# Shorter mean sums, split last tiles, reordered first products and identity products in the norms of an f32 kernel

## The reference, cut to what matters

```python
def rms_norm(x, g):
    x32 = x.astype(jnp.float32)
    y = x32 * lax.rsqrt(jnp.mean(x32 * x32, axis=-1, keepdims=True) + EPS)
    return (y * g.astype(jnp.float32)).astype(x.dtype)
...
        x = x + mixed @ w_out[l]
        x = x + peer_ffn(rms_norm(x, norm2_g[l]), w_peer_q[l], peer_keys1[l], peer_keys2[l],
                         peer_u[l], peer_v[l])
```

## Time and profile before

| what | value |
|---|---|
| median of 3 runs | 2213.49 us (2211.61 to 2214.72) |
| the profiled execution's own time | 2211.12 us |
| its span, first to last instruction | 2209.3 us |
| mean granted PE clock | 0.977 of full speed |
| PE busy | 2133.0 us, 97% of the span |
| DVE, ACT busy | 1543.1 us, 1127.5 us |
| PE on the chain that ended last | 85% |

### The profile page before, as it was taken

The page is one execution under the profiler, slowest core; times in us unless marked ns, Lnnn a source line. Parts: engine busy times, 40 slices in busy tenths (PEclk is TensorE's granted clock), DMA queues, the critical chain, the costliest instruction groups (busy, mean ns, idle before and its releaser), DMA issues.

```text
span 2209.3 us, 40301 instructions
## 1 busy us (share of the span) xinstructions
PE 2133.0 (97%) x16826; PEld 2059.7 (93%) x16826; DVE 1543.1 (70%) x2684; ACT 1127.5 (51%) x1745; POOL 274.4 (12%) x256
## 2 busy tenths in 40 slices
PE   8999999999999999999999999999999999989998
PEld 7888899999998999999999999999879999989998
DVE  6777588764996777877777576573457886676664
ACT  5556578544444666554444454562245543435553
POOL 0000000001889445410000000000000000000000
PEclk9999999999999999999999999999899999999999
DMA  5433433566554444446777676322015767544563
GB/s 194 160 130 108 137 124 109 188 219 229 182 182 163 146 143 142 138 162 241 246 236 265 219 243 236 114 95 87 25 39 189 245 234 252 198 146 153 182 180 116
DMA packets 104005, 375.43 MB, mean 170 GB/s; under 512 B 11536, under 2 KB 12176, under 8 KB 103184
## 3 DMA queue, kind: packets, MB, share of 16 engines
q1 hardware_dynamic: 103824, 372.86, 50.2%
HBM read 370.71 MB, written 2.10 MB: 169 GB/s over the span
## 4 chain that ended last, share of the span: by engine, by line
PE 85%; DVE 7%; ACT 3%; POOL 2%; DMA 1%; issue 1%; SPq 0%; DVEq 0%; ACTq 0%
PE ps L365 24%; PE ps L366 23%; PE ps L367 23%; PE ps L696 3%; DVE wl L1428 2%; POOL wl L2117 2%; PE ps L449 1%; PE ps L495 1%; DMA raw<-in_ada 1%; PE ps L433 1%; PE ps L434 1%; PE ps L435 1%; PE ps L790 1%; PE ps L809 1%; ACT wh L997 1%
## 5 line engine op out<-in xcount | busy, mean ns | idle before, releaser
L365 PE MATMUL ps<-xah,wh 128*128 128x256 f32 x2944 | 850.9, 289 | 15.6 <-DVE xal L1453 5.2
L366 PE MATMUL ps<-xal,wh 128*128 128x256 f32 x2944 | 838.7, 285 | 0.0
L367 PE MATMUL ps<-xah,wl 128*128 128x256 f32 x2944 | 838.4, 285 | 0.0
L1428 DVE TENSOR_TENSOR wl<-raw,wh 128x1024 fp32r<-128x1024 f32 (+2 forms) x548 | 644.6, 1197 | 216.2 <-ACT wh L997 215.0
L997 ACT ACTIVATE wh<-raw 128x1024 fp32r<-128x1024 f32 (+1 forms) x608 | 620.1, 1036 | 300.2 <-PE ps L367 179.5
L365 PEld LDWEIGHTS ps<-xah,wh 128*128 128x128 f32 x2944 | 570.9, 194 | 27.7 <-issue 18.3
L366 PEld LDWEIGHTS ps<-xal,wh 128*128 128x128 f32 x2944 | 570.9, 194 | 0.5 <-issue 0.2
L367 PEld LDWEIGHTS ps<-xah,wl 128*128 128x128 f32 x2944 | 570.2, 194 | 0.0
L365 PE MATMUL ps<-hh,wh 128*128 128x256 f32 x1024 | 291.7, 285 | 9.5 <-DVE wl L1428 7.8
L366 PE MATMUL ps<-arenar,wh 128*128 128x256 f32 x1024 | 289.7, 283 | 0.0
L367 PE MATMUL ps<-hh,wl 128*128 128x256 f32 x1024 | 289.7, 283 | 0.0
(11 more groups left out here) (332 smaller groups left out, 2942.3 us busy)
## 6 DMA issues: line engine op xcount, KB each, us to landing
raw<-in_pu SPq DMA_DIRECT2D x128, 512.0 KB, 3.3
raw<-in_pv SPq DMA_DIRECT2D x128, 512.0 KB, 3.6
raw<-in_ada SPq DMA_DIRECT2D x96, 512.0 KB, 4.2
raw<-in_ff_up SPq DMA_DIRECT2D x88, 512.0 KB, 3.6
raw<-in_w_xbc SPq DMA_DIRECT2D x32, 512.0 KB, 3.3
raw<-in_ff_down SPq DMA_DIRECT2D x32, 512.0 KB, 3.7
raw<-in_w_z SPq DMA_DIRECT2D x16, 512.0 KB, 3.3
raw<-in_w_so SPq DMA_DIRECT2D x16, 512.0 KB, 4.1
```

Of the source, the lines that this page charges most:

```text
L365: mm(o, w0, x0, start=start, stop=False, skip_group_check=skip)
L366: mm(o, w0, x1, start=False, stop=False, skip_group_check=skip)
L367: return mm(o, w1, x0, start=False, stop=stop, skip_group_check=skip)
L1428: tt_(W.lo(i), W.raw(i), W.hi(i).bitcast(f32), ALU.subtract).then_inc(S["lowV"], 1)
```

## The change

In each norm:

- `sums` (new, DVE): slices 0 to 5 of the squares are added into slice 0 by three additions (512, 512 and 256 columns). The first is put ahead of the residual additions of tile 2, the other two ahead of those of tile 3. `mean` then multiplies only slices 0, 6 and 7: 6 matmuls, 12 records.
- `last_two` (new, PE): for `out`, `down` and `oo` the last tile's halves go to two banks, each with a signal of its own. DVE adds and ACT squares slice 6 when half 0 is full, slice 7 when half 1 is. The calls of `lows` and `halves` that belong to a bank are now made once for each half.
- `first_tiles` and `l0` issue the six products that need only the high half of a slice first, behind a wait for ACT, then the three with the low half, behind the wait for DVE.
- `keep` (new, PE): products of the identity with itself, written to a part of a bank that is not read: 2 behind slice 0 of the mean (not in nc), 3 ahead of the wait for the reciprocal and 7 ahead of the first tiles (not in nc, l0; in fin only the 2 and the 3).

```diff
+            def last_two(key, w, c, nk, x, need, between=iter(())):
+                for half in range(2):
+                    P = take((key, half))
...
+                    last.then_inc(B.full((key, half), len(W.units)), 1)
...
+            def keep(P, n, start=True):
+                for _ in range(n):
+                    mm(P[:, 256:384], ident, ident, start=start, stop=True, skip_group_check=True)
...
-                for k in range(8):
-                    t.wait_ge(*step_of(name, "sq", k))
+                for k in (0, 6, 7):
+                    t.wait_ge(*(step_of(name, "sq", k) if k else summed(name)))
...
+                    if k == 0:
+                        keep(P, idle, False)
...
             def stat(name, J, sq, ids=range(8)):
-                mean(name, J, sq, ids)
-                row(name, ids)
+                mean(name, J, sq, ids, 2)
+                row(name, ids, 3)
...
+                keep(P, 7)
                 for k in range(8):
-                    need(k)
+                    need_h, need_x = need
+                    need_h(k)
                     for n, (o, i, hi, lo) in enumerate(u):
-                        last = product(o, hi[:, k, :], lo[:, k, :], x[0][:, k, :], x[1][:, k, :], k == 0 and n != 1, k == 7, skip=True)
+                        mm(o, hi[:, k, :], x[0][:, k, :], start=k == 0 and n != 1, stop=False, skip_group_check=True)
+                        mm(o, lo[:, k, :], x[0][:, k, :], start=False, stop=False, skip_group_check=True)
+                    need_x(k)
+                    for n, (o, i, hi, lo) in enumerate(u):
+                        last = mm(o, hi[:, k, :], x[1][:, k, :], start=False, stop=k == 7, skip_group_check=True)
...
+            mean("l0", K1024, sqx, HIGH, 2)
...
+                if i == 3 and (key, 0) in B.units:
+                    for half in range(2):
+                        halves(B.units[key, half] + AHEAD)
+                        a.wait_ge(*B.is_empty((key, half)))
+                        square(name, 6 + half, x, sq)
...
+            def sums(name, sq, i):
+                if i == 2:
+                    v.wait_ge(*step_of(name, "sq", 3))
+                    tt_(sq[:, 0:2], sq[:, 0:2], sq[:, 2:4], ALU.add).then_inc(own.up(), 1)
+                if i == 3:
+                    v.wait_ge(*step_of(name, "sq", 5))
+                    v.wait_ge(own.sem, own.n)
+                    tt_(sq[:, 0:2], sq[:, 0:2], sq[:, 4:6], ALU.add).then_inc(own.up(), 1)
+                    v.wait_ge(own.sem, own.n)
+                    tt_(sq[:, 0], sq[:, 0], sq[:, 1], ALU.add).then_inc(S["norm_sum"], 1)
...
             for j in range(4):
                 P = B[("y", j)]
                 v.wait_ge(*B.is_full(("y", j)))
+                sums("l0", sqx, j)
```

More of the change, by code:

```diff
@@ L394, in tile @@
                 W.done[i] = B.is_full(key)
+            def last_two(key, w, c, nk, x, need, between=iter(())):
+                for half in range(2):
+                    P = take((key, half))
+                    for k in range(0, nk, 8):
+                        n = min(8, nk - k)
+                        i, hi, lo = unit((key, half, k), w, c + half, k * 128, n * 128, 128)
+                        for q in range(n):
+                            need(k + q)
+                            last = product(P[:, 0:256], hi[:, q, :], lo[:, q, :], x[0][:, k + q, :], x[1][:, k + q, :],
+                                           k + q == 0, k + q == nk - 1)
+                        if k + n < nk:
+                            last.then_inc(W.used(i), 1)
+                        if half == 0:
+                            next(between, None)
+                    last.then_inc(B.full((key, half), len(W.units)), 1)
+                    W.done[i] = B.is_full((key, half))
             def quarters(key, w, c, xs=None):
@@ L450, in mean, with row @@
                                   stop=k == 7, skip_group_check=True)
+                    if k == 0:
+                        keep(P, idle, False)
                 last.then_inc(B.full((name, "stat"), len(W.units)), 1)
-            def row(name, ids=range(8)):
+            def row(name, ids=range(8), idle=0):
                 P = take((name, "row"), ids)
+                keep(P, idle)
                 t.wait_ge(S["rstd"], NORMS.index(name) + 1)
@@ L497, in modulation, with slices @@
                     yield
+            def slices(name):
+                return tuple((lambda k, what=what: t.wait_ge(*step_of(name, what, k))) for what in ("h", "x"))
             def n1(k):
@@ L515, in pe @@
                 if i == 0:
-                    first_tiles((("qk", 0), "w_q", 0), (("qk", 1), "w_q", 2), XA, n1, range(6))
+                    first_tiles((("qk", 0), "w_q", 0), (("qk", 1), "w_q", 2), XA, slices("n1"), range(6))
                 elif i > 1:
@@ L645, in pe @@
             for i in range(4):
-                tile(("out", i), "w_out", 2 * i, 8, XA, mixed, between=mo)
+                (tile if i < 3 else last_two)(("out", i), "w_out", 2 * i, 8, XA, mixed, between=mo)
             W.mark("spill")
@@ L763, in pe @@
             for k in range(8):
+                t.wait_ge(*step_of("l0", "h", k))
+                for n, (o, i, hi, lo) in enumerate(u):
+                    mm(o, hi[:, k, :], XA[0][:, k, :], start=k == 0 and n < 2, stop=False, skip_group_check=True)
+                    mm(o, lo[:, k, :], XA[0][:, k, :], start=False, stop=False, skip_group_check=True)
                 l0(k)
                 for n, (o, i, hi, lo) in enumerate(u):
-                    last = product(o, hi[:, k, :], lo[:, k, :], XA[0][:, k, :], XA[1][:, k, :], k == 0 and n < 2, k == 7, skip=True)
+                    last = mm(o, hi[:, k, :], XA[1][:, k, :], start=False, stop=k == 7, skip_group_check=True)
                     if k == 7:
@@ L962, in ffn @@
                 for i in range(4):
-                    tile(("down", l, i), "ff_down", 8 * l + 2 * i, 22, XF, gated, between=late)
+                    (tile if i < 3 else last_two)(("down", l, i), "ff_down", 8 * l + 2 * i, 22, XF, gated, between=late)
             ffn(0)
@@ L1522, in dve @@
             v.wait_ge(S["ld_cst"], 16)
+            for i in (2, 3):
+                sums("n1", sq1, i)
             norm("n1", xT, lambda k: pc("norm1", k), hbuf, XA)
@@ L2069, in ffn @@
                 gated(21)
-                residual([("down", l, i) for i in range(4)], l, 40, range(0, 22, 8))
+                residual(after, [("down", l, i) for i in range(4)], l, 40, range(0, 22, 8))
             ffn(0, "od")
@@ L2100, in dve @@
             v.wait_ge(own.sem, own.n)
-            residual([("oo", i) for i in range(4)], 1, 16)
+            residual("f1", [("oo", i) for i in range(4)], 1, 16)
             ffn(1, "fin")
```

61 lines of the change are left out of this document (36 added, 25 removed).

## The result

| | before | changed |
|---|---|---|
| median of the runs | 2212.21 us (2205.46 to 2214.72, 7 runs) | 2204.71 us (2201.65 to 2206.36, 7 runs) |
| profiled execution, own time | 2211.12 | 2206.36 |
| its span | 2209.3 | 2204.5 |
| its mean granted clock of TensorE | 0.977 | 0.982 |

The ratio is 0.9969, interval 0.9959 to 0.9978: faster by 0.31%, 6.9 us by the ratio, 7.5 us by the medians and 4.8 us between the two profiled executions, of which the changed kernel's is the slowest of its seven. The forecast sum was -4.0.

What follows compares the result with a forecast made beforehand. PE, busy 97% of the span, was taken as the bound, so only its gaps and slow stretches could be won. The terms sum to -4.0 us: 2207.1 from the profiled 2211.12, or 2209.5 against the median 2213.49; range 2203 to 2219.

Steps and rivals of the forecast that it cites:

- n1: Norm n1: the keeps give back the shorter mean's 0.7 us, and 3.2 us of slow products are helped: 1.0 us faster.
- n2: Norm n2: late last square puts row matmuls 3.4 us later, the part behind them gives back 1.4: 2.0 us slower.
- The stretch behind the row: From row matmuls through slow products in n2, f0, od, f1: 4.9 us becomes 3.5, so 1.4 us gained each.
- nc: Norm nc: 20 fewer mean records, 2.3 us, and 1.7 of slow products: 4.0 us faster, bounds -1 and -5.
- l0: Norm l0: sums delay the squares, row matmuls +3.9 us, high halves first give back 0.6: 3.5 slower, bounds 2 and 4.5.
- od: Norm od: row matmuls 1.05 us later behind late squares, the part behind them gives back 1.4: 0.35 us faster.
- f1: Norm f1: shorter mean, no table load, row matmuls 0.35 us earlier, and 1.4 gained behind them: 1.75 us faster.
- f0: Norm f0: table load still ends last, row matmuls 0.25 us later, 1.4 gained behind them: 1.15 us faster.
- fin: Norm fin: no weights left to convert, square root at 2200.5 instead of 2201.74: 1.25 us faster, all on the path.
- the identity products do not raise the clock: Rival, at the norms: identity products only stand in PE's queue, total 7.4 us slower, 2221 us; chance 0.20.
- the clock does not fall: Rival: keeps and pairs fill the wait in f1 and part of od, no slow records there, 2205 us; chance 0.13.
- the halves do not wait for each other: Rival: halves done ahead of slice 6, n2 and od lose nothing, 4.5 us and part of l0, 2203 us; chance 0.10.

Runs made afterwards that it cites:

- the repeat: The unchanged changed kernel timed again in a later series against the kernel before: ratio 0.9961, interval 0.9947 to 0.9974.
- the second execution: Another profiled execution of the changed kernel, with nothing edited, taken in the repeat: 2204.7 us.
- nc alone: The kernel before, with only norm nc's mean shortened by the three sums: 2207.95 us, ratio 0.9979.
- the keeps alone: The kernel before, with only identity products added, 3 ahead of the row matmuls and 7 behind: 2208.15 us, ratio 0.9989.
- version six: The changed kernel with the last tile's halves made up front, l0's sums behind its additions and no keeps in l0's mean: 2194.29 us, ratio 0.9923.

## Why the prediction came out right, and where its steps did not

The time, 2204.71 against a forecast of 2209.5 and a range of 2203 to 2219, lay inside. The forecast was hung on a median of 2213.49 from three runs, and seven gave 2212.21. The comparison of profiled executions, -4.8 against -4.0, looks closer than it is: by the ratios of all runs it is -6.9, and -8.6 in the repeat, so the gain was forecast at about half its size. It fell into the class faster by over 0.2%, which had 0.43. Of the signs named ahead, the n2 square came 2.6 us after the old one (3.6 said), the two halves stood between the additions, l0 had its gaps, nc had full clock behind it, and the spacing of the 14 keep records shrank within them in f1 and f0 (0.16 and 0.15 on the mean), but not in od and n2 (0.20; in the second execution 0.18 and 0.13). By steps:

- **n1, -1.0 forecast, -1.0 and -0.4 measured.** The row matmuls came 0.4 later (15.65 to 16.04), the first product 0.5 later, and 3.3 us of slow products behind it were gone.
- **n2, +2.0 forecast, +2.3 and +0.8 measured.** Row matmuls 3.4 us later were forecast; they came 2.6 later, 3.0 against the last product. The stretch behind the row was to give 1.4; it gave 0.7 in the first execution and 2.2 in the second. The step was "the clock should rise that much sooner, mostly within the keeps". In the first execution it failed: PE worked without a pause from the last mean records at 488.94, as the step said, and yet the spacing halved only at 495.94, 7.0 us later and 0.3 us before the old 496.26, so the keeps ended at +3.7, not +3.4, and a microsecond of products was still slow. In the second execution, with the same instructions, the rise fell among the keeps and no product was slow. The step took as fixed what differs from execution to execution.
- **nc, -4.0 forecast, -5.3 and 4.6 measured.** The records gave their 2.6 us (4.03 - 1.40), against 2.3 in the sum. For the clock the step took "two thirds: 1.7"; no product behind was slow, so all of the 2.6 was won. The step had taken two thirds as its hedge where the effect was whole.
- **l0, +3.5 forecast, +4.2 and +4.0 measured.** The last square came 5.9 us behind the last product (1377.78 to 1383.68), against 2.96 before, the three of the step; the row matmuls came 4.2 us later (11.0 - 6.8), near its 3.9. The 6.8 is at the low end of what the old code does (8.5 in "nc alone"), so the loss is at the high end. The head start of the high halves was to give 0.6 back. This is the step of the prediction that failed outright: 12 context products stand behind the row matmuls, and in the kernel before the first product on a slice (1388.56) followed the last of them (1388.20) at 0.36 us, only 0.24 over the spacing. From the row matmuls to that product it is 2.54 us now and was 2.69. Elsewhere the two runs with the low halves awaited show no gain from the head start that can be told from 2 us; there the keeps stand in front.
- **od, -0.35 forecast, -1.0 measured, twice.** Row matmuls +0.9 against the last product (1886.75 to 1888.34, less 0.7), forecast +1.05. The stretch behind gave 1.9 instead of 1.4: the slow products had lasted 6.1 us (1889.67 to 1895.76), which at 0.44 is 2.7 us lost, and each norm had been given the mean price of 2.0.
- **f1, -1.75 forecast, -3.2 measured, twice.** The row matmuls came 1.4 us earlier, 1.1 against the last product, where 0.35 was forecast, and the stretch behind gave 2.1 instead of 1.4; here the slow products had lasted 5.3 us, 2.3 lost. This is the term that was sized worst.
- **f0, -1.15 forecast, -0.9 and -1.0 measured.** The row matmuls were late by 0.1 (0.25 forecast); the first product came 3.2 behind them, against 2.95 before, at full clock.
- **fin, -1.25, measured -1.3** by the last product ahead of the norm (2197.95 and 2194.43) and the row matmuls:

```profile
2197.52 0.71 PE L487 MATMUL ps<-cst,small 128*128 128x128 f32 x4 [0.35 <-DVE small L1500]
```

- **Stretches without a term.** +0.5 and +2.15 around n2, -1.4 between f0 and od. Between n2 and nc PE waits for the low halves of weights, 6.6 us in all before, 8.5 after and 7.2 in the second execution. Between f0 and od a slow stretch of products shrank from 5.9 to 3.9 us; in "the keeps alone", where that code is unchanged, it is 4.5, so a part of this is not the change. Neither was tried by a run of its own. They cancelled in part, as did terms that were too small and too large; a sum that is right to 0.8 us with unforeseen terms of 1 to 2 us is in part luck.

**The rivals.** That the identity products do not raise the clock is refuted by the run without them (and by version six without them). The case for it had come from the Trainium skill, "TensorE: Matmul & The Clock Gate", Part 4, which says that products in transpose mode do not count as activity in the same way; the traces here show that plain identity products count. That the clock does not fall came true in nc alone; in f1 it was half true, since the keeps still took 0.16 a record. In the version with halves up front it is true in od and f1, in version six in f1 alone. That the halves do not wait for each other was false in this kernel, and true in the version that moves them up front: that was worth 3.5 to 5 us (0.9945 against 0.9961 and 0.9969), where the rival had been priced at 4.5 for n2 and od. But part of it came by the clock that did not fall in od and f1, which that rival did not have.

## What to carry to other kernels

Price a wait on the matrix engine twice: the wait itself, and what its clock then costs the products behind it. Filler work paid most in combination with a short wait: identity products at the norms brought 2.4 us in all, if anything, where the waits stayed as they were, and 7.2 where the last squares came early. Before adding a reduction step to the engine that delivers the last operand, see what is queued behind it there: in l0 the sums cost about 2 us in front of the additions, and the filler products in front of the last operand's records another 0.9. Behind the additions, without these fillers, nothing was lost that can be told. And profile the same kernel twice before reading a stage to better than a microsecond.

## What the runs showed of the hardware that was not expected

- The clock fell with PE busy all the time. Between products, in nc, it stood at 0.52 behind the 32 one-column records of the mean, 4.03 us, and at 1.00 behind 12 of them, 1.40 us. In the kernel with keeps alone it was 0.59 over 2000 to 2004 and 0.50 behind, though PE had gone from products into the 32 records and on into the identity products without a pause.
- Where the clock falls or rises differs between executions of the same code. In l0 the old mean's 32 records took 3.70 us in the kernel before and 5.16 in the kernel with nc's sums only; in n2 the changed kernel's 14 keep records took 0.20 us each in one execution and 0.13 in another.
- An identity product's record takes 0.12 us at full clock, and 0.20 (14 in a row) to 0.24 (6 in n2, 489.82 to 491.24) at half.
- The table load starts right behind ACT's last square, before the mean it serves is there, and takes 1.28 us. In n2 it ended at 490.19 and the root began at 490.20: with the mean shortened, it is the load that ends last, and only an earlier last square would help.
